# One raw place of a weight stream given up for a fifth place of split units, in a two-layer hybrid encoder

## The reference

```
h = rmsnorm(x); proj = h @ w_in[l]                    # 2048 -> 6144: q, k, v, B, C, u
attention: 8 heads, rotary q and k, softmax of two score maps, w = p0 - lam * p1, w @ v, rmsnorm
convolution: B * conv3(C * u)
x = x + concat(attention, convolution) @ w_out[l]     # 2048 -> 2048
h = rmsnorm(x)
x = x + (silu(h @ w_gate[l]) * (h @ w_up[l])) @ w_down[l]   # 2048 -> 5632 twice, 5632 -> 2048
```

## Time and profile before

| | us |
|---|---|
| median of 3 runs | 2184.16 (2184.01 to 2184.34) |
| the profiled execution | 2183.82 |
| its span, first to last instruction | 2182.0 |
| TensorE matmuls busy | 2168.0 |
| VectorE busy | 1780.7 |
| ScalarE busy | 1206.4 |
| mean DMA rate | 195 GB/s, 425 MB moved |

### The profile page before, as it was taken

One profiled execution on the slowest core, in us unless ns is written; L12 is line 12 of the kernel. 1 busy time (PEld: TensorE's weight loads), 2 busy tenths in 40 slices (PEclk: granted clock), 3 DMA queues, 4 the chain that ended last, 5 costly groups with the idle time before them and its releaser, 6 DMA issues.

```text
span 2182.0 us, 27513 instructions
## 1 busy us (share of the span) xinstructions
PE 2168.0 (99%) x10481; PEld 1808.1 (83%) x10481; DVE 1780.7 (82%) x2139; ACT 1206.4 (55%) x1646; POOL 129.8 (6%) x154
## 2 busy tenths in 40 slices
PE   9999999999999999999999999999999999999998
PEld 7888888788888888888888888887888888888886
DVE  6776676899999998888866667769999999888887
ACT  6445564556556555555544555545655565555554
POOL 0031120000000000000001212200000000000000
PEclk9999999999999999999999999999999999999999
DMA  9654455545654565455566545554456456545554
GB/s 350 209 176 172 167 174 174 207 160 189 232 197 174 204 225 182 181 215 198 214 207 209 177 155 174 176 188 177 174 210 227 162 187 235 196 174 215 190 194 172
DMA packets 118307, 425.29 MB, mean 195 GB/s; under 512 B 13600, under 2 KB 14240, under 8 KB 117792
## 3 DMA queue, kind: packets, MB, share of 16 engines
q1 hardware_dynamic: 115344, 416.40, 53.9%
q0 software_dynamic: 1536, 4.20, 0.8%
q10 hardware_dynamic: 1296, 2.94, 0.4%
HBM read 417.20 MB, written 2.10 MB: 192 GB/s over the span
## 4 chain that ended last, share of the span: by engine, by line
PE 96%; DVE 2%; ACT 1%; issue 0%; POOL 0%; DMA 0%; ACTq 0%; DVEq 0%
PE bank L1653 18%; PE bank L1655 17%; PE bank L1654 17%; PE bank L1627 14%; PE bank L1630 7%; PE bank L1665 7%; PE bank L1667 7%; PE bank L1666 7%; PE bank L1818 1%; PE bank L1777 1%; PE bank L1800 1%; DVE wlo L1001 0%; DVE wlo L994 0%; PE bank L1756 0%; POOL o_rms L555 0%
## 5 line engine op out<-in xcount | busy, mean ns | idle before, releaser
L604 ACT ACTIVATE whi<-raw 128x1024 fp32r<-128x1024 f32 x596 | 626.0, 1060 | 469.5 <-PE bank L1655 284.2
L994 DVE TENSOR_TENSOR wlo<-raw,whi 128x1024 fp32r<-128x1024 f32 x596 | 724.5, 1232 | 163.5 <-ACT whi L604 150.5
L610 ACT ACTIVATE whi<-raw 128x1024 fp32r<-128x1024 f32 x368 | 345.7, 952 | 233.0 <-PE bank L1655 167.6
L1001 DVE TENSOR_TENSOR wlo<-raw,whi 128x1024 fp32r<-128x1024 f32 x368 | 390.7, 1088 | 44.7 <-ACT whi L610 40.8
L1627 PE MATMUL bank<-xg,whi 128*128 128x512 f32 x1280 | 406.9, 399 | 0.6 <-DVE wlo L1226 0.6
L1653 PE MATMUL bank<-whi,xg 128*128 128x512 f32 x1024 | 402.7, 393 | 0.0
L1655 PE MATMUL bank<-whi,xg 128*128 128x512 f32 x1024 | 399.1, 390 | 0.0
L1654 PE MATMUL bank<-wlo,xg 128*128 128x512 f32 x1024 | 398.9, 390 | 0.0
L1630 PEld LDWEIGHTS bank<-xg,wlo 128*128 128x128 f32 x1280 | 240.4, 188 | 56.9
L1630 PE MATMUL bank<-xg,wlo 128*128 128x256 f32 x1280 | 252.1, 278 | 0.0
L1655 PEld LDWEIGHTS bank<-whi,xg 128*128 128x128 f32 x1024 | 192.2, 188 | 40.1
(11 more groups left out here) (157 smaller groups left out, 2680.5 us busy)
## 6 DMA issues: line engine op xcount, KB each, us to landing
raw<-w_gu_dram SPq DMA_DIRECT2D x352, 512.0 KB, 5.4
raw<-w_in_dram SPq DMA_DIRECT2D x188, 512.0 KB, 4.5
raw<-w_down_dram SPq DMA_DIRECT2D x176, 512.0 KB, 5.2
raw<-w_out_dram SPq DMA_DIRECT2D x64, 512.0 KB, 4.4
swapped<-qk POOLq DMA_DIRECT2D x32, 128.0 KB, 2.7
x_t<-x_t_dram SPq DMA_DIRECT2D x8, 256.0 KB, 6.6
raw<-w_in_dram SPq DMA_DIRECT2D x8, 256.0 KB, 5.8
resid<-x_dram SPq DMA_DIRECT2D x2, 1024.0 KB, 15.8
```

Of the source, the lines that this page charges most:

```text
L604: act.activation(whi[:, blk.slot(k)], raw[:, slot, half * UNIT_KT:(half + 1) * UNIT_KT, :], ACT.Copy).then_inc(hi_ready, 1)
L610: act.activation(whi[:, quad.slot(n), 0:tiles.stop - tiles.start], raw[:, quad.raw(), tiles, :], ACT.Copy).then_inc(hi_ready, 1)
L994: dve.tensor_tensor(wlo[:, blk.slot(k)], raw[:, slot, half * UNIT_KT:(half + 1) * UNIT_KT, :], lo_bits(whi[:, blk.slot(k)]), ALU.subtract) ...
L1001: dve.tensor_tensor(wlo[:, quad.slot(n), into], raw[:, quad.raw(), tiles, :], lo_bits(whi[:, quad.slot(n), into]), ALU.subtract).then_inc( ...
```

## The change

One place of `raw` goes and one slot of `whi` and `wlo` comes; the memory used is the same, 8 KB of each partition going from the one to the other. FINAL_UNITS keeps its value, 3. The instructions of every engine and their order stay the same; what changes is which place and slot each uses, and the numbers waited for: a load waits for the last split of the load three before it, no longer four, and a split for the product of the split five before it, no longer four.

```
--- before
+++ after
@@ -33,10 +33,10 @@
 UNIT_KT = 2
 LOAD_KT = 2 * UNIT_KT
-NRAW = 4
-NSPLIT = 4
-
-FINAL_UNITS = NSPLIT - 1
+NRAW = 3
+NSPLIT = 5
+
+FINAL_UNITS = 3
 UNITS = KT // UNIT_KT
```

## The result

The changed kernel takes 2262.99 us (median of 4 runs, 2262.26 to 2264.17) against 2184.09 (median of 4): 3.62% more, ratio 1.0362, 95% interval 1.0344 to 1.038. The forecast was 2255, with a range of 2232 to 2280. Its profiled execution has a span of 2260.5 us, 78.5 more than before.

A forecast was written before the change was run, and what follows sets the result against it. TensorE, busy 99%, bounds the kernel; with three places, loads held by quads come late. Added to 2183.8 us, 58.5 (18 gate/up pairs), 7.6 (first pairs) and 4.5 (down pairs), 71 in all, give 2255 us, range 2232 to 2280.

The forecast's parts named there:

- G: Gate/up load of left 6 and 7; claimed to wait for the second quad's place, TensorE then 3.25 us late in all.
- F: Gate/up load of left 5 and right 5; claimed to wait for the first quad's place (q0), making TensorE wait 1.7 us.
- The link, 6.08 us: From a place's release through issue, 3.6 us landing, ScalarE and VectorE steps to TensorE's product: 6.08 us.
- The fifth slot, 0.5 us back: In gate/up pairs the extra slot lets VectorE end the first quad 0.5 us sooner; bounds 0 and 1.36.
- A pair, 3.25 us: Each of 18 gate/up pairs with three quads, behind each layer's first, loses 3.25 us: 58.5 us.
- First pairs, 7.6: First gate/up pair of each layer, without gain from the slot, loses 3.8 us, twice: 7.6 us.
- Down pairs, 4.5: Down pair 1's loop takes 10.68 us against TensorE's 10.20 per turn: 2.25 us per layer, 4.5 in both; pair 0 loses 0.
- 1: Rival: the fifth slot gives a whole slot, the first quad ending 1.36 us sooner; 2237 us, chance 0.05.
- 2: Rival: loads land at the median, 5.4 us, adding 1.8 to each link; 2349 us, chance 0.04.
- 3: Rival: the loads stay hidden and no product waits; 2184 us, chance 0.03.
- 4: Rival: faster, as TensorE's pauses for low halves vanish; 2180.5 us, chance 0.01.
- Rival 5: TensorE's clock falls in the new waits, 1.45 us for each of 40, adding 58; 2313 us, chance 0.03.

The follow-up runs named there:

- e2: Kernel before (four places, four slots) plus one wait: F waits for the first quad's fourth split in gate/up pairs with three quads; 2243.48 us, ratio 1.027.
- e5: Kernel before plus one wait: in down pair 1 a turn's load waits for the fourth split of the previous turn's quad; 2190.06 us, ratio 1.0027.
- e6: Changed kernel (three places, five slots) with the second quad's second products moved ahead of left 5 and right 5 on all engines; 2185.78 us, ratio 1.0006.
- e1: Kernel before with three places instead of four and still four slots, on chip 1; 2267.99 us, ratio 1.0382.
- e4: Kernel before plus two waits: F waits for the first quad's fourth split, G for the second quad's; 2262.82 us, ratio 1.036.
- e10: Kernel before with three places instead of four and still four slots, on chip 12; 2273.59 us, ratio 1.0413.
- e9: Changed kernel run again without any edit, on chip 12; 2259.86 us, ratio 1.0348.
- e7: Three places and four slots, with the second quad's second products moved ahead of left 5 and right 5; 2191.51 us, ratio 1.0032.

## Why the prediction was right

*What bounds it, and where a place is short.* Right. The new waits stand in the 20 gate/up pairs with three quads and in down pair 1, none in the last pair of a layer, in down pair 0 or in a plain stage. e2 to e5 make them one by one, and e6 takes those of gate/up away without giving back the place. Of the signs named ahead, two were off in size: TensorE's visible wait for G is 1.0 to 1.3 us (once 1.6) and not 1.5 to 2, and ScalarE waits 217 us for w_gu loads and not 100, as it idles 4.0 us before F's first half and 4.7 before G's; it is not the bound engine, and this costs nothing by itself.

*The link, 6.08 us.* Right within 0.04 where it can be read. Its landing, 3.6 us, was the row of one load; in the changed kernel the first halves of F took 3.56 to 3.83. SyncE had been held, as forecast, and the median over all w_gu loads fell from 5.4 to 4.6:

```profile
raw<-w_gu_dram SPq DMA_DIRECT2D x352, 512.0 KB, 4.6
```

So the far end, 5.4, was not a number of the held loads. That it came from loads behind others in the queue fits this fall, but was not tested by itself. The rule of the Trainium skill (SBUF — State Buffer, the DMA setup-cost knee), 3.2 us, was too short here by 0.4 to 0.6: no first half of F landed under 3.5 in the changed kernel.

*The fifth slot, 0.5 us back.* Right. In pair 5 q0's place came free at 637.18, that is 617.02 if the 20.16 us that TensorE was late until then are taken off: 0.45 sooner than 617.47. The mean of the 18 pairs is 0.46, and the first pairs have 0, as forecast.

*A pair, 3.25 us.* Mis-sized by 0.24. The 18 pairs took 62.7 us together, 3.49 each. The first halves of F and of G landed after 3.68 us on average in them and not 3.6, which is 0.15 for the two links. What was left out is the slow start of TensorE after the wait for G, 0.1. That after the wait for F costs nothing more, since G's release hangs on VectorE and not on TensorE.

*First pairs, 7.6.* They took 8.8: 3.7 in layer 1, as forecast, and 5.1 in layer 0, where the first half of G landed after 4.9 us and not 3.6; that is the whole excess. The clock fell too, after the pause before left 5, but this added nothing: TensorE had to wait for G afterwards all the same. From the timeline and the windows of the changed kernel:

```profile
411.02 0.50 PE L1653 MATMUL bank<-whi,xg 128*128 128x512 f32 x1 [2.04 <-DVE wlo L994]
411.36 0.40 PE L1654 MATMUL bank<-wlo,xg 128*128 128x512 f32 x1
411.59 0.59 PE L1655 MATMUL bank<-whi,xg 128*128 128x512 f32 x1
411.99 0.63 PE L1653 MATMUL bank<-whi,xg 128*128 128x512 f32 x1
412.41 0.63 PE L1654 MATMUL bank<-wlo,xg 128*128 128x512 f32 x1
```

```profile
411.00:415.00 4.00, 3.98 (x11) 3.12 (x12) 3.96 (x5) 2.43 (x3) 0.00 (x0) 0.58 0.00 0
```

Starts 0.42 us apart instead of 0.227: half speed.

*Down pairs, 4.5.* They took 6.6; the loop was right, its landing 0.14 too short on average over the seven turns of each layer.

*The sum.* 58.5 + 7.6 + 4.5 became 62.7 + 8.8 + 6.6, and 0.3 at the start, which is no part of the change (e2 to e5, with four places, start 0.2 to 0.5 us later than the profile before). 8 us of 79 were missing, 6 of them in landings (2.7 in the 18 pairs, 1.3 in the first, 1.9 in down), 1.8 in the slow starts.

*The rivals.* 1 lies inside the range and is ruled out by the slot's 0.46 us where it said 1.36, not by the time; 2 failed by its size, 3 and 4 because the kernel got slower. Rival 5 did not happen as priced in the changed kernel, where the clock fell once, but its mechanism is real: e1, e2, e4 and e10, whose waits for F are 1.8 to 2.3 us and not 1.5 to 1.75 as in most pairs of the changed kernel, had 7 or 8 falls each.

## What to carry to other kernels

What decides whether a buffer is deep enough is not the number of its places but the time between a release and the use that needs it; look for the item that holds its place longest, take its release from the timeline, and add one link (issue, landing, each engine's step) to it. Where that comes too late, moving work of the bound engine into the gap can be worth more than memory: here q1's second products, moved ahead of two units on all engines, won back 77 of 79 us. Two such waits in a row can cost more than the two alone, because the engine between them hands the delay of the first on to the second; here that was some 0.4 us of 3.8 per pair.

## What was not expected of the hardware

- The granted clock of TensorE fell to half (1.2 GHz), for 3.4 us each time, after pauses of only 1.8 to 2.3 us between full-speed stretches, with the fall 0.0 to 1.5 us after work had begun again. It did not follow every such pause: of 84 pauses of 1.8 to 2.3 us (between 380 and 2150 us, in all twelve profiles), 31 were followed by a fall, and of 111 pauses of 1.0 to 1.8 us none. The length alone does not decide: the three longest pauses had no fall either (2.30 and 2.41 us in e10, 2.62 in e9). What else decides was not tried. The product behind the longest, and the window from there on, in e9:

```profile
425.10 0.50 PE L1653 MATMUL bank<-whi,xg 128*128 128x512 f32 x1 [2.62 <-DVE wlo L994]
...
425.00:430.00 5.00, 4.90 (x21) 4.05 (x22) 4.88 (x6) 4.55 (x6) 0.00 (x0) 1.00 1.00 377
```

- What a fall costs depends on what follows. In e2, with one pause per pair, it cost 1.5 us; in e10, where a wait for a load follows in the same pair, a pair with a fall took only 0.1 to 0.2 us more than one without: its wait for G is gone, since TensorE came later to a load that was late anyway. One window of e10:

```profile
552.00:557.00 5.00, 4.22 (x12) 3.35 (x13) 4.96 (x7) 2.70 (x3) 0.00 (x0) 0.66 0.00 0
```

- The landing of the same 512 KB, when SyncE had been held, differed by 0.1 to 0.2 us between profiles: F's first half took 3.52 to 3.56 us on average in e1, e2 and e4 (chip 1), 3.56 and 3.55 in e6 and e7 (chip 5), 3.63 and 3.67 in e9 and e10 (chip 12); in the down stage it was 3.3 to 3.6 in e5 and 3.6 to 4.0 in the changed kernel. This is enough to move this kernel by several us: three places and four slots took 2268.0 us on chip 1 and 2273.6 on chip 12. Comparing the changed kernel's first runs with e1 hid two thirds of what the fifth slot gives (5 us seen, 13.7 on one chip). One profile per run does not show whether the chip is the cause.
